# Spreading 1/denominator over the head rows: the repeated reciprocal as stationary operand, the identity as moving operand

## The reference, cut to what matters

```python
s = jnp.einsum('nlhd,nmhd->nhlm', q, km).astype(jnp.float32) * ATTN_SCALE
p = jax.nn.softmax(s, axis=-1)
return jnp.einsum('nhlm,nmhd->nlhd', p, vm.astype(jnp.float32))
```

## Time and profile before

| what | us |
|---|---|
| median of 3 runs (lowest, highest) | 1087.69 (1084.55, 1089.52) |
| the profiled execution, its own time | 1084.03 |
| its span in the trace | 1082.2 |
| TensorE busy in the span | 970.9 (90%) |
| VectorE busy | 346.7 (32%) |
| ScalarE busy | 272.6 (25%) |
| GpSimd busy | 151.1 (14%) |

### The profile page before, as it was taken

One profiled execution on the slowest core, in us unless ns is written; L12 is line 12 of the kernel. 1 busy time (PEld: TensorE's weight loads), 2 busy tenths in 40 slices (PEclk: granted clock), 3 DMA queues, 4 the chain that ended last, 5 costly groups with the idle time before them and its releaser, 6 DMA issues.

```text
span 1082.2 us, 16454 instructions
## 1 busy us (share of the span) xinstructions
PE 970.9 (90%) x6540; PEld 748.2 (69%) x6540; DVE 346.7 (32%) x743; ACT 272.6 (25%) x580; POOL 151.1 (14%) x242
## 2 busy tenths in 40 slices
PE   6999999968989998799997379999999999999575
PEld 6999889834655555478885368778878878877331
DVE  5202110176546555835444800010001001001056
ACT  5202110034334444812222011111111111111054
POOL 0000000422112212400000012112112211211000
PEclk9999999999999999989998579999999999999787
DMA  9999996599667566096215939999899999991354
GB/s 333 328 365 320 377 333 257 216 274 312 247 244 246 176 216 208 13 337 233 78 64 178 332 101 326 302 316 319 298 297 317 321 311 327 325 322 38 136 213 150
DMA packets 116281, 273.42 MB, mean 253 GB/s; under 512 B 13984, under 2 KB 82080, under 8 KB 113408
## 3 DMA queue, kind: packets, MB, share of 16 engines
q1 hardware_dynamic: 107456, 247.97, 66.8%
q0 software_dynamic: 8768, 24.66, 6.5%
HBM read 256.33 MB, written 95.30 MB: 325 GB/s over the span
## 4 chain that ended last, share of the span: by engine, by line
PE 81%; DVE 8%; issue 4%; DMA 3%; ACT 3%; POOL 1%; SPq 0%; DVEq 0%; POOLq 0%; ACTq 0%
PE psum L642 76%; PE psum L701 4%; DMA back<-pair_d 1%; DVE front L1476 1%; ACT front L1092 1%; POOL back L1611 1%; DVE back L1208 1%; PE psum L845 1%; DMA middle<-pair_d 0%; DVE middle L1240 0%; DVE middle L1562 0%; DMA back<-h_d,back 0%; DMA back<-w_in 0%; DVE middle L1241 0%; DMA pair_d<-front,back 0%
## 5 line engine op out<-in xcount | busy, mean ns | idle before, releaser
L642 PE MATMUL psum<-back,front 128*64 128x128 f32 (+2 forms) x1280 | 149.9, 302 | 11.5 <-DVE back L490 7.9
L642 PEld LDWEIGHTS psum<-back,front 128*64 128x64 f32 (+2 forms) x1280 | 108.8, 164 | 45.9 <-issue 30.8
L642 PE MATMUL psum<-front 64*128 64x512 f32 (+5 forms) x448 | 120.5, 506 | 12.1 <-DVE stats L1208 7.4
L642 PE MATMUL psum<-back 128*128 128x112 f32 (+3 forms) x1152 | 123.1, 307 | 2.2 <-issue 2.0
L642 PEld LDWEIGHTS psum<-back 128*128 128x128 f32 (+1 forms) x1152 | 111.8, 170 | 14.5 <-issue 8.8
L642 PE MATMUL psum<-back,middle 128*128 128x112 f32 (+1 forms) x880 | 101.8, 316 | 1.7 <-issue 1.7
L642 PE MATMUL psum<-x_high,w_high 128*128 128x352 f32 x288 | 94.1, 327 | 8.3 <-DVE w_low L358 8.3
L642 PEld LDWEIGHTS psum<-back,middle 128*128 128x128 f32 (+1 forms) x880 | 91.3, 181 | 14.5 <-issue 14.5
L642 PEld LDWEIGHTS psum<-front 64*128 64x128 f32 (+2 forms) x448 | 51.5, 191 | 66.1 <-issue 48.3
L642 PE MATMUL psum<-x_low,w_high 128*128 128x352 f32 x288 | 93.4, 324 | 0.0
L642 PE MATMUL psum<-x_high,w_low 128*128 128x352 f32 x288 | 93.2, 324 | 0.0
(11 more groups left out here) (186 smaller groups left out, 1237.7 us busy)
## 6 DMA issues: line engine op xcount, KB each, us to landing
out_win_k_s<-cache_win_k SPq DMA_DIRECT2D x16, 2044.0 KB, 13.9
out_win_v_s<-cache_win_v SPq DMA_DIRECT2D x16, 2044.0 KB, 13.4
front<-w_down SPq DMA_DIRECT2D x16, 1024.0 KB, 7.6
middle<-w_gate SPq DMA_DIRECT2D x16, 1024.0 KB, 6.6
back<-w_up SPq DMA_DIRECT2D x16, 1024.0 KB, 8.6
back<-winkT SPq DMA_DIRECT2D x8, 1792.0 KB, 7.9
back<-cache_win_v SPq DMA_DIRECT2D x8, 1024.0 KB, 6.7
front<-w_gate SPq DMA_DIRECT2D x8, 1024.0 KB
```

The source lines that it names most:

```text
L642: return nc.tensor.matmul(out, lhsT, rhs, start=start, stop=stop, skip_group_check=True)
```

## The change

VectorE's reciprocal now writes its result 64 times: its input is the two sums with a repeat of 64 on the inner axis, and its output `RDW` is 128x(2x64). The spreading products take `RDW` of a head as stationary operand (128x64) and the identity as moving operand (128x128), in place of ones (128x64) and the diagonal matrix (128x128). They wait for `s_rd` directly. GpSimd's 96 scalings with their waits are gone, with the semaphore `s_dg`. `RDW` has two buffers, so VectorE now waits before it writes one for the products of the unit two before it.

```diff
-        DG = [at(50768 + 2 * P * s, 2, P) for s in range(2)]
+        RDW = [at(50768 + 2 * HD * s, 2, HD) for s in range(2)]
...
-                    pe.wait_ge(s_dg, u + 1)
+                    pe.wait_ge(s_rd, u + 1)
                     for s in range(2):
-                        last = mm(b[64 * s:64 * s + 64, P:2 * P], ones[:, 0:HD], DG[u % 2][:, s, :], True, True)
+                        last = mm(b[64 * s:64 * s + 64, P:2 * P], RDW[u % 2][:, s, :], ident, True, True)
                     last.then_inc(s_O, 1)
...
                 dve.wait_ge(s_exp, 2 * u + 2)
-                V_.reciprocal(RD[:, 2 * u:2 * u + 2], DEN[:, 2 * u:2 * u + 2]).then_inc(s_rd, 1)
+                if u >= 2:
+                    dve.wait_ge(s_O, u - 1)
+                V_.reciprocal(RDW[u % 2], DEN[:, 2 * u:2 * u + 2].unsqueeze(2).broadcast_to([P, 2, HD])).then_inc(s_rd, 1)
...
-            for u in range(NU):
-                pool.wait_ge(s_rd, u + 1)
-                if u >= 2:
-                    pool.wait_ge(s_O, u - 1)
-                for s in range(2):
-                    last = G.tensor_scalar(DG[u % 2][:, s, :], ident, RD[:, 2 * u + s:2 * u + s + 1], None, ALU.mult)
-                last.then_inc(s_dg, 1)
```

More of the change, by code:

```diff
@@ L245, in build @@
         s_S, s_min, s_exp = sem("s_S"), sem("s_min"), sem("s_exp")
-        s_rd, s_dg, s_inv = sem("s_rd"), sem("s_dg"), sem("s_inv")
+        s_rd, s_inv = sem("s_rd"), sem("s_inv")
         s_T, s_Td, s_Ta, s_PV, s_O, s_OB = sem("s_T"), sem("s_Td"), sem("s_Ta"), sem("s_PV"), sem("s_O"), sem("s_OB")
```

## The result

The changed kernel takes 1099.15 us (median of 5 runs, 1089.95 to 1100.33). The kernel before, run beside it on the same chip, takes 1084.55 us (median of 5, 1083.20 to 1089.52). The ratio is 1.0119, with a 95% interval of 1.0088 to 1.0150, so the change costs 1.2%, about 12.9 us. The forecast had the direction right, and nearly twice the size: 24.2 us. The time lies at the low end of the range, where I had put a flatter slope and fewer stalls.

What follows compares the result with a forecast made beforehand. TensorE was taken to bound mid-windowed units, VectorE units 40 to 45. Terms 5.0 + 9.2 + 4.7 + 5.3 + 0 = 24.2 us, added to 1087.7, gave 1111.9 us; 8-in-10 range 1098 to 1127.

Steps and rivals of the forecast that it cites:

- The bound and the mechanism: Attention: TensorE bounds mid-windowed units, VectorE units 40 to 45; longer reciprocals delay minima and `o_out`, half of 48 us counts.
- The price of the reciprocal: VectorE, 48 times: 128x128 reciprocal takes 1.15 us, 1.0 us longer each, from slopes of 7.5 or 8.4 ns an element.
- the gift of the last two: Units 46 and 47: removing GpSimd gives back what two longer reciprocals cost, 2.0 us, so sum 0.
- the 1.8 us of gaps in units 37 to 39: Memory units 37 to 39: 3.0 us of longer reciprocals meet some 1.8 us of gaps, leaving 1.2 us.
- The windowed units: Groups 0 to 3: short units pay, gaps hide the rest; 5.0 us in group 0, 9.2 us in groups 1 to 3.
- Units 31 to 39: Forecast for units 32 to 39: waits for `o_out` less gaps, 4.7 us, bounds nothing and 8.
- Units 39 to 45: Forecast for units 40 to 45: VectorE bounds; 6.0 us added less 0.74 us free time, 5.3 us.
- Units 46 and 47: End of attention: cost and gift cancel, sum 0; tail after unit 46's reciprocal stays about 5.1 us.
- the products: TensorE's 192 spreading products keep number and shape at 277 ns; swapping their operands costs nothing.
- the new wait: VectorE's wait for products of unit `u-2` costs nothing, already met by the program's order.
- the cheap reciprocal: Rival: reciprocal costs about a scaling, 0.285 us; 1080 to 1089 us; chance 0.05 faster, 0.05 no change.
- the full price: Rival: whole price reaches the path, 1138 us, or 1126 with three quarters; chance 0.2 for 1122 us and more.

Runs made afterwards that it cites:

- late: Changed kernel with the same 128x128 reciprocal moved behind the unit's copies, minima and `o_out` on VectorE; 1088.84 us against 1085.23 us for the kernel before, ratio 1.0035.
- both pairs: Kernel before and changed kernel, each profiled twice, on two chips; the stretches between `o_out(0)` and `o_out(47)` are 14.3 us longer after in either pair.
- pool_copy: Kernel before with operands swapped and GpSimd spreading the 128x2 reciprocal by one copy; ratio 0.9961 to the kernel before, 0.9996 when repeated.
- half: Changed kernel with the reciprocal writing 32 of 64 repeats per head (128x64); reciprocal 0.39 us dearer than before; whole kernel 1727.96 us, only the attention is read.
- pool_dummy: Changed kernel plus two GpSimd scalings per unit into a scratch tile nobody reads in time; 1101.31 us, ratio 1.0144 to the kernel before.

## Why the prediction was wrong in size

**The bound and the mechanism** were right, with one omission below (units 39 to 45). VectorE pays, TensorE's extra step waits for `o_out` in the short units, and the large units hide it. Unit 21 shows the second, in VectorE's timeline of the changed kernel:

```profile
350.86 0.94 DVE L1223 RECIPROCAL back<-stats 128x128 f32<-128x128 f32 x1
...
352.14 1.23 DVE L1208 CUSTOM_DVE_ANT_0 back<-psum,back 128x1024 f32<-128x1024 f32 x1 [0.34 <-PE psum L642]
```

The gap of 1.12 us has shrunk by 0.78 to 0.34 us, the reciprocal's whole price, and the minimum comes no later for it. `late` shows it by experiment: without the bad place the windowed units cost nothing.

**The price of the reciprocal** is the step that failed: 1.15 us taken, 0.944 measured, so 0.79 instead of 1.0 us for each unit. I carried the slope from two and nine elements on to 128, fourteen times the end of its base, where the 15 ns by which the nine-element row lies high make the slope 1.2 to 2.1 ns an element too steep: 7.5 or 8.4 against 6.25. The low end of my range had a slope of 5.8, and that was the nearer one. The kind is right, several times a simple operation's price for an element, as a scaling of 128 elements takes 285 ns; but the repeat count of 8 that the Trainium skill gives ("VectorE: DVE Perf Modes") and I turned into 8 ns an element isn't in the trace, and the measurement of 6.25 decides. With 0.79 in place of 1.0 the forecast's own sum would have been 18.5.

Cut to the rows of the first table, which hold the reciprocals 2 to 47, the forecast reads as below. Unit 0's 1.0 us lies ahead of the first `o_out`, which starts anywhere between 221.8 and 224.9 us in the kernels of this study, so it can't be judged.

| units | forecast | the same with 0.79 for 1.0 | measured, both pairs |
|---|---|---|---|
| 0 to 31 | 4.0 + 9.2 + 1.0 = 14.2 | 11.2 | 10.5, 9.2 |
| 31 to 39 | 4.7 - 1.0 + 0.9 = 4.6 | 3.6 | 2.4, 3.6 |
| 39 to 45 | 4.4 + 1.0 = 5.4 | 4.1 | 3.0, 3.0 |
| 45 to 47 | 1.0 - 2.0 = -1.0 | -1.2 | -1.6, -1.6 |
| all | 23.2 | 17.7 | 14.3, 14.3 |

The third column scales what the units pay, and keeps the gaps of units 40 to 45 and the gift of the last two as they were. So 5.5 of the 8.9 us that are missing are the price of the reciprocal; with the 1.8 us of gaps in units 37 to 39 kept as well it is 5.9. The other 3.0 to 3.4 are gaps and hand-overs, read in the rows below and not tested one by one.

**The windowed units** come out as forecast once the price is right. In units 16 to 31, where nothing else moves, I had 0.95 + 1.0 for units 18 and 19, 0.8 for 20, 2.8 for the last group and 1.0 for unit 32, together 6.55; times 0.79 that is 5.2, and 4.76 was measured. The patterns of the earlier trace rows hold. The row of units 8 to 16 had 2.8 us, 2.2 at the right price, and 2.0 was measured at equal clock. For group 0 the two pairs give 5.3 and 2.5 us, because the clock moves the kernel before by 2.7 us; at equal clock it is about 3.4 us (the estimate above), where the forecast for these reciprocals, 4.0 and 0.85 for unit 8, comes to 3.8.

**Units 31 to 39** I had named as the part argued with the least, and at equal clock it is one of the two furthest off: 2.4 us measured, 3.6 forecast at the right price (3.2 with the gaps of units 37 to 39 kept). Which of its gaps took in more wasn't looked into. The 3.6 of the second pair holds 1.2 us of lower clock and is no hit.

**Units 39 to 45.** I had named VectorE alone as the bound there. The earlier trace rows gives ScalarE the same 14.96 us, and the runs show that before the change the two were even: in `pool_copy` VectorE's busy time from `o_out(39)` to `o_out(45)` is 14.24 us where it was 14.54, ScalarE's is 14.70, and the stretch takes 15.22 us where it took 15.25. VectorE's free time went into waits for ScalarE. Only the change makes VectorE the bound alone, with 18.29 of 18.29 us. The 1.1 us between 4.1 and 3.0 has a place in VectorE's rows. VectorE is now without a gap, as the row of the stretch shows beside the last of the earlier trace rows:

```profile
453.90:469.60 15.70, 10.68 (x100) 6.53 (x96) 15.70 (x29) 12.94 (x35) 0.00 (x0) 1.00 0.01 2
```

Two units follow each other in 6.19 us, 3.1 each and not 3.6, and it was 4.99. Unit 44 of the pair, first before, then after:

```profile
448.55 0.15 DVE L1221 RECIPROCAL stats<-stats 128x2 f32<-128x2 f32 x1
448.62 0.40 DVE L1211 TENSOR_REDUCE stats<-psum 128x1 f32<-128x256 f32 x1
448.94 0.27 DVE L1229 TENSOR_TENSOR middle<-psum,back 128x128 f32<-128x128 f32 x1
449.14 0.41 DVE L1211 TENSOR_REDUCE stats<-psum 128x1 f32<-128x256 f32 x1
449.47 1.34 DVE L1345 TENSOR_TENSOR wo_low<-back,wo_high 128x1024 fp32r<-128x1024 f32 x1
450.74 0.15 DVE L1221 RECIPROCAL stats<-stats 128x2 f32<-128x2 f32 x1
```
```profile
463.45 0.94 DVE L1223 RECIPROCAL back<-stats 128x128 f32<-128x128 f32 x1
464.31 0.36 DVE L1211 TENSOR_REDUCE stats<-psum 128x1 f32<-128x256 f32 x1
464.59 0.27 DVE L1231 TENSOR_TENSOR middle<-psum,back 128x128 f32<-128x128 f32 x1
464.78 0.41 DVE L1211 TENSOR_REDUCE stats<-psum 128x1 f32<-128x256 f32 x1
465.11 1.21 DVE L1347 TENSOR_TENSOR wo_low<-back,wo_high 128x1024 fp32r<-128x1024 f32 x1
466.25 0.94 DVE L1223 RECIPROCAL back<-stats 128x128 f32<-128x128 f32 x1
```

To the start of the last row it is 2.19 us and 2.80 us, 0.61 more instead of 0.79. The split occupies VectorE for 1.27 us before and 1.14 after (start to start), and the first minimum 0.32 and 0.28. The other unit of the pair gains in the same way 0.03 and 0.04 us, and a gap of 0.11 us goes ahead of its split, which is part of the 0.74 us that I had deducted.

The two gains have different reasons. The shorter minimum belongs to the long reciprocal ahead of it and not to GpSimd: the 32 minima read 389 ns on the mean in the changed kernel, 388 in `half` and 387 in `pool_dummy`, where GpSimd works, but 409 before, 410 in `pool_copy` and 411 in `late`, where no long reciprocal stands right ahead of them. The longer split is one of the two that GpSimd's pair seems to hold. In `pool_copy`, where GpSimd makes a short copy in place of two scalings, seven of the eight splits read 1.21 to 1.23. But then VectorE waits longer, 0.16 and 0.17 us, for ScalarE ahead of the splits of units 43 and 45, where it was 0.11:

```profile
454.04 1.23 DVE L1345 TENSOR_TENSOR wo_low<-back,wo_high 128x1024 fp32r<-128x1024 f32 x1 [0.16 <-ACT wo_high L1038]
```

So the longer splits cost next to nothing before (15.25 against 15.22 us), and their shortening counts only where VectorE is the bound. That it was GpSimd that lengthened these two splits is read from the rows and not tested by itself.

**Units 46 and 47.** Forecast: the tail after unit 46's reciprocal stays at 5.1 us. Measured: 4.27 us, where it was 5.08, so a gift of 0.8 us; with the right price I would have had 0.4. VectorE's rows after:

```profile
469.64 0.94 DVE L1223 RECIPROCAL back<-stats 128x128 f32<-128x128 f32 x1
470.50 0.22 DVE L1231 TENSOR_TENSOR middle<-psum,back 128x128 f32<-128x128 f32 x1
470.65 1.21 DVE L1347 TENSOR_TENSOR wo_low<-back,wo_high 128x1024 fp32r<-128x1024 f32 x1
471.78 0.94 DVE L1223 RECIPROCAL back<-stats 128x128 f32<-128x128 f32 x1
472.64 0.22 DVE L1231 TENSOR_TENSOR middle<-psum,back 128x128 f32<-128x128 f32 x1
472.78 1.21 DVE L1347 TENSOR_TENSOR wo_low<-back,wo_high 128x1024 fp32r<-128x1024 f32 x1
473.91 0.28 DVE L1231 TENSOR_TENSOR middle<-psum,back 128x128 f32<-128x128 f32 x1
```

I had seen that the gaps go, and that is what the rows show: seven instructions without a gap. I had put the second reciprocal at 456.1, 2.6 us behind the first; it stands 2.14 us behind. Of the 0.4 us between the two, 0.2 is its price, and the rest is in `o_out` and the split, which read 0.22 and 1.21 us here. The 0.22 us, 0.27 before, are again those of an instruction right behind the long reciprocal.

**The clock, the products, the new wait.** The products were right at nothing, the wait on `s_O` too: in 48 units VectorE's idle time ahead of the reciprocal is 0.3 us, none of it put down to TensorE. The clock did move, by more than some of the terms, but between executions of one kernel as well, so the runs don't show whether the change itself lowers it anywhere. Of the rivals, the cheap reciprocal is excluded by 944 ns, and the full price by the gap in unit 21 and by the sum: 14.3 of the 37.8 us that VectorE has more reach the end, where it asked for three quarters. `half` shows what the second had right: gaps are used up as the price grows, so the last tenths cost more than the first.

## What to carry to other kernels

Don't let an expensive operation write a repeated result: take it once on the small tile and repeat it by a copy, here 156 + 227 ns instead of 944 ns. Put what nobody waits for soon behind what others wait for in an engine's order; that alone gave back 9 of 13 us, but nothing where the engine is saturated. A slope from nine elements isn't a price at 128: ask at both ends of the slope, and give the sum as a range of it. Compare a stretch only with one at the same granted clock, and look at the busy time of all engines before one is called the bound.

## What the runs showed of the hardware

- VectorE's fp32 reciprocal took 144 ns + 6.25 ns an element a partition, from 2 to 128 elements, from 8 on with a repeated input. A copy with the same repeated input took 227 ns for 128 elements.
- GpSimd took 290 ns for a 128x128 copy with repeated input and 612 ns for a scaling of that size.
- Two GpSimd scalings of 128x128 took 1.18 us alone and 2.23 us beside a VectorE instruction with two operands in SBUF. That instruction took 1.21 us there, and 1.34 and 1.35 us at two places where it began 0.67 and 0.68 us into the pair, which then took its usual 1.19 us.
- VectorE's instruction right behind a long reciprocal read shorter than behind a short one: 0.36 against 0.40 us for a minimum over 128x256, 0.22 against 0.27 us for a 128x128 multiplication.
- The granted clock from the first to the ninth `o_out` was 0.97 and 0.87 in two executions of the same kernel, and the same 312 products with all that goes with them took 48.92 and 51.67 us.
- The final layer norm took 36.3 or 42.9 us in two executions of the changed kernel. Eight products in it took 3.4 to 3.7 us at a granted clock of 1.00 (the changed kernel's first execution) and 6.2 to 6.5 us at 0.56 to 0.59 (its second). What decides between the two isn't shown.
